# Gating unit's bias in two rounded parts, and the second layer's scan queries on 512 tokens, in a four-layer transformer kernel

## The reference, cut to what matters

```python
def sgu(pu, pv, ln_g, ln_b, w_s, b_s):
    vn = layer_norm(pv, ln_g, ln_b).reshape(B, nch, SGU_CHUNK, SGU_GROUPS, SGU_GROUP_DIM)
    mixed = jnp.einsum('gts,bnsgc->bntgc', w_s, vn) + b_s.T[None, None, :, :, None]
    return pu * mixed.reshape(B, N, SGU_WIDTH)

def gla_heads(...):
    q = heads(pq, GLA_DK) * (GLA_DK ** -0.5)
    k = heads(pk, GLA_DK)
...
    oc_f, s_f = gla_scan(qcg, kcg, vcg, gfc, zeros)
    ol_f, _ = gla_scan(qlg, klg, vlg, gfl, s_f)
```

## Time and profile before

| | |
|---|---|
| median of 3 runs | 3522.41 us (3520.08 to 3523.33) |
| the profiled execution: its time | 3518.86 us |
| its span, first to last instruction | 3516.7 us |
| mean granted clock of TensorE | 0.947 of full speed |
| TensorE busy | 3188.0 us, 91% of the span |
| VectorE, ScalarE, POOL busy | 54%, 34%, 6% |
| DMA | 321.84 MB, mean 92 GB/s |

### The profile page before, as it was taken

The page is one execution under the profiler, slowest core; times in us unless marked ns, Lnnn a source line. Parts: engine busy times, 40 slices in busy tenths (PEclk is TensorE's granted clock), DMA queues, the critical chain, the costliest instruction groups (busy, mean ns, idle before and its releaser), DMA issues.

```text
span 3516.7 us, 43743 instructions
## 1 busy us (share of the span) xinstructions
PE 3188.0 (91%) x18216; PEld 2645.0 (75%) x18216; DVE 1906.8 (54%) x2789; ACT 1178.4 (34%) x1763; POOL 208.4 (6%) x144
## 2 busy tenths in 40 slices
PE   7997889999988889999898999988998888997997
PEld 6886778888877667777777878756887777775776
DVE  7756555665434755777454443574434544457543
ACT  4234341221232544222342333253221534425322
POOL 0003100000010000000002120000001012100001
PEclk9999999999989999999899999999999799999997
DMA  5543123333211003555221123102113112320221
GB/s 203 178 154 126 55 78 126 121 131 120 84 55 60 1 13 121 179 176 177 88 86 69 65 75 110 42 1 81 54 66 96 71 66 88 103 81 7 97 94 58
DMA packets 91373, 321.84 MB, mean 92 GB/s; under 512 B 10070, under 2 KB 11991, under 8 KB 90025
## 3 DMA queue, kind: packets, MB, share of 16 engines
q1 hardware_dynamic: 81236, 289.43, 24.4%
q10 hardware_dynamic: 9940, 29.61, 2.3%
HBM read 297.26 MB, written 21.74 MB: 91 GB/s over the span
## 4 chain that ended last, share of the span: by engine, by line
PE 77%; DVE 10%; ACT 8%; issue 4%; DMA 1%; ACTq 0%; POOL 0%; SPq 0%; POOLq 0%; DVEq 0%
PE PS L384 76%; ACT whi L195 2%; ACT Pq L1274 1%; DVE STs L1311 1%; PE PS L387 1%; ACT nt L611 1%; DVE JUNK L514 1%; DVE stage L514 1%; DVE STq L1311 1%; DVE wlo L209 1%; ACT Ps L1274 1%; DMA Ht<-in_hT 1%; ACT U L616 0%; DVE fg L721 0%; ACT Ht L2304 0%
## 5 line engine op out<-in xcount | busy, mean ns | idle before, releaser
L384 PE MATMUL PS<-U,whi 128*128 128x512 f32 (+1 forms) x5408 | 1178.0, 363 | 93.7 <-DVE U L641 27.9
L384 PEld LDWEIGHTS PS<-U,whi 128*128 128x128 f32 x5408 | 913.8, 193 | 283.2 <-issue 59.3
L209 DVE TENSOR_TENSOR wlo<-stage,whi 128x1024 fp32r<-128x1024 f32 x339 | 417.0, 1232 | 1060.7 <-ACT whi L195 1060.1
L195 ACT ACTIVATE whi<-stage 128x1024 fp32r<-128x1024 f32 x339 | 358.3, 1058 | 1425.7 <-PE PS L384 1403.5
L384 PE MATMUL PS<-U,wlo 128*128 128x512 f32 (+1 forms) x2704 | 620.9, 355 | 0.0
L384 PE MATMUL PS<-Y,whi 128*128 128x512 f32 (+1 forms) x2240 | 582.9, 364 | 18.9 <-DVE Y L723 12.9
L384 PEld LDWEIGHTS PS<-U,wlo 128*128 128x128 f32 x2704 | 458.1, 189 | 79.7
L384 PEld LDWEIGHTS PS<-Y,whi 128*128 128x128 f32 x2240 | 397.3, 191 | 93.8 <-DVE Y L723 14.8
L384 PE MATMUL PS<-Y,wlo 128*128 128x512 f32 (+1 forms) x1120 | 367.7, 363 | 0.0
L384 PEld LDWEIGHTS PS<-Y,wlo 128*128 128x128 f32 x1120 | 208.9, 191 | 35.0
L384 PE MATMUL PS<-whi,U 128*128 128x512 f32 (+2 forms) x832 | 223.6, 359 | 11.3 <-DVE mV L1046 6.4
(11 more groups left out here) (412 smaller groups left out, 3279.3 us busy)
## 6 DMA issues: line engine op xcount, KB each, us to landing
stage<-in_w SPq DMA_DIRECT2D x128, 512.0 KB, 3.3
stage<-in_ada SPq DMA_DIRECT2D x80, 512.0 KB, 3.3
stage<-in_adb SPq DMA_DIRECT2D x48, 512.0 KB, 3.2
stage<-in_p_mg SPq DMA_DIRECT2D x16, 512.0 KB, 3.2
stage<-in_p_ma SPq DMA_DIRECT2D x16, 512.0 KB, 3.4
stage<-in_p_ms SPq DMA_DIRECT2D x16, 512.0 KB, 3.5
stage<-in_wo SPq DMA_DIRECT2D x16, 512.0 KB, 3.2
GS<-FS ACTq DMA_DIRECT2D x20, 384.0 KB
```

What stands on the lines that cost most here:

```text
L195: act.activation(self.parts[r % n][0], self.stage[i % len(self.stage)], ACT.Copy).then_inc(*self.S.up("w_hi", i))
L209: dve.tensor_tensor(lo, self.stage[i % len(self.stage)], hi.bitcast(F32), ALU.subtract).then_inc(*self.S.up("w_lo", i))
L384: return pe.matmul(o, l, r, start=start, stop=stop_, skip_group_check=True)
```

## The change

The bias is split once in each layer, into a rounded upper part (`BH`, by ScalarE) and the rest (`BL`, by VectorE); a row of ones is rounded too (`ONE`). The bias products then are taken over all four (or two) chunks of a bank at once, by a moving operand that repeats the group's 128 values: per group 2 + 2 rounded products of 512 and 256 columns in place of 6 plain ones of 128 in the first layer, and 2 of 512 in place of 4 in the second. The raw bias `B` moves to another place in memory. In the second layer, the query tiles j = 0 and 1 are projected and copied for 512 tokens, not 768.

```diff
@@ pe_gla @@
-                pe_proj(pe, T(f"p_gqk{L}", j), xU, True, ("g_qk", L, j))
+                pe_proj(pe, T(f"p_gqk{L}", j), xU, j >= 2 or G.full, ("g_qk", L, j))
@@ act_gla @@
-                act.activation(G.QK[:, j, :], B.of(i)[:, 0:TOK], ACT.Copy, scale=0.125 if j < 2 else 1.0).then_inc(
+                N = G.N if j < 2 else TOK
+                act.activation(G.QK[:, j, 0:N], B.of(i)[:, 0:N], ACT.Copy, scale=0.125 if j < 2 else 1.0).then_inc(
@@ Gating @@
-                self.B = place(n + "sb", [1, 4, 128], F32, offY2 + 18432)
+                self.BL = place(n + "sl", [1, 4, 128], F32R, offY2 + 18432)
+                self.B = place(n + "sb", [1, 4, 128], F32, offZ + 18432)[:, :, :]
+                self.BH = place(n + "sh", [1, 4, 128], F32R, offY2 + 20672)
+                self.ONE = place(n + "one", [1, 128], F32R, offY2 + 22720)
@@ pe_sgu @@
-                    pe.wait_ge(*at("sgu_in2", L))
+                    pe.wait_ge(*at("v_bias", L, 1))
+                    pe.wait_ge(*at("v_blo", L))
                 for c in range(G.nc):
                     mm(pe, s[:, 128 * c:128 * c + 128], G.V[:, c, 128 * g:128 * g + 128], G.W[:, g, :], c % 4 == 0, False)
-                    last = mm(pe, s[:, 128 * c:128 * c + 128], ONES[0:1, :], G.B[0:1, g, :], False, False)
+                for a, b in cols(G.full):
+                    for part in (G.BH, G.BL):
+                        last = mm(pe, s[:, a:b].rearrange("p (c e) -> p c e", e=128), G.ONE[0:1, :],
+                                  part[0:1, g:g + 1, :].to_broadcast([1, (b - a) // 128, 128]), False, part is G.BL)
@@ act_sgu @@
+            act.wait_ge(*at("sgu_in2", L))
+            act.activation(G.ONE[:, :], ONES[0:1, :], ACT.Copy).then_inc(*up("v_bias", L, 0))
+            act.activation(G.BH[:, :, :], G.B, ACT.Copy).then_inc(*up("v_bias", L, 1))
@@ dve_sgu @@
+            dve.wait_ge(*at("v_bias", L, 1))
+            dve.tensor_tensor(G.BL[:, :, :], G.B, G.BH[:, :, :].bitcast(F32), ALU.subtract).then_inc(*up("v_blo", L))
             dve.wait_ge(*at("w_used", T(f"p_sv{L}", 3)))
```

More of the change, by code:

```diff
@@ L52 @@
     "modulated": ("n_mul", "u_mod"), "gain": ("n_gain", "u_gain"), "rows_act": ("m_va", "g_va"),
-    "rows_dve": ("m_vd", "g_vd", "s_v", "q_v"), "v_norm": ("v_st", "v_ag", "v_rr", "v_n", "v_n1", "v_n2"),
+    "rows_dve": ("m_vd", "g_vd", "s_v", "q_v"), "v_norm": ("v_blo", "v_st", "v_ag", "v_rr", "v_n", "v_n1", "v_n2"),
     "qk_norm": ("q_rr", "q_nz"), "sigmoid": ("cb_sig", "cb_moved", "b_sig", "q_gs", "v_sig", "g_sig", "m_o"),
@@ L2520, in sp_program @@
                 sp.dma_start(V.W[:, :, :], A[f"sgu_w{L}"]).then_inc(*dma("sgu_in1", L))
-                sp.dma_start(V.B[:, :, :], A[f"sgu_b{L}"]).then_inc(*dma("sgu_in2", L))
+                sp.dma_start(V.B, A[f"sgu_b{L}"]).then_inc(*dma("sgu_in2", L))
                 sp_merge(sp, "s", L, N)
```

## The result

| | before | after |
|---|---|---|
| median, same chip | 3522.41 us (3518.55 to 3524.79, 5 runs) | 3496.17 us (3493.66 to 3500.01, 5 runs) |
| ratio | | 0.9927, 95% interval 0.9917 to 0.9938 |
| the profiled execution: its time | 3518.86 us | 3493.66 us |
| its span | 3516.7 us | 3491.7 us |
| mean granted clock | 0.947 | 0.951 |

A forecast was written before the change was run, and what follows sets the result against it. The prediction took TensorE's queue (77% of the chain) and its dipping clock as the bound. It summed 12.0 + 12.8 - 1.7 + 5.8 = 28.9 us, giving 3493.5 us from the median 3522.41, range 3485 to 3506.

The forecast's parts named there:

- small products at full clock: Gating units of both layers: cheaper bias products take 7.2 + 4.8 = 12.0 us off TensorE's queue.
- clock in the gating places: Half clock costs 15.9 us in four gating stretches; 12.8 us gained, with one fall left in the first layer's pair.
- wait behind the last pairs: Merge's fourth slice waits for VectorE's two serial groups: 0.7 us first layer unless a fall stays, 1.7 us second.
- query tiles: Second layer's scan start, j = 0 and 1: dropping the 256-column half saves 2.89 us twice, 5.8 us.
- untouched stretches: Elsewhere in the program: clock falls may shift either way by one or two of 3 us; not in the sum.
- I go by the row: Gating units: a removed plain product priced at the profile's 0.415 us, gaining 12.0 us, not 4.7 by the four-pass rule.
- the low bound: New one-row bias products priced like rounded products with 128 partitions: 0.234 us for 512 columns; high bound 0.99.
- The slower rival: One-partition rounded products run at the plain rate, 0.99 us for 512 columns: 3.6 us slower, 3526; chance 0.03.
- one fall of 3.1 us: First layer's last pair of groups: one clock fall assumed to remain, lowering the clock gain from 15.9 to 12.8 us.
- The rival in which the falls stay: Gating stretches: clock still falls as before, perhaps 5 of 15.9 us gained, 3500.6, at worst 3505; chance 0.28.
- The reason I gave, less time in small products: First layer's groups 0 and 1: 2.4 us of small products, down from 4.9, should no longer lower the clock.
- New work on ScalarE and VectorE: Bias copies and subtraction before the normalisation: cost nothing given 1.08 us of cover; under 1 us without it.

The follow-up runs named there:

- other profiles: The kernel before and the changed kernel, each run and profiled once more unedited: 3522.93 us and 3493.01 us.
- 64 rows in turn with 128: Kernel before, each bias product replaced by a plain 128-column product with a 64-row stationary operand, bias left out: 3510.1 us, one run.
- the rounded parts chunk by chunk: Changed kernel, its rounded bias parts added as two one-row products of 128 columns after each product with `V`: 3521.89 us, one run.
- The run with the moved group: Changed kernel, the third group's mixing product placed between the last group's two tiles in both layers: 3489.23 us, ratio to before 0.9899.
- the order alone: Kernel before, same plain products, but a group's bias products placed after all its products with `V`: 3501.97 us, ratio to before 0.9932.
- wide plain products: Kernel before, unrounded bias taken over four or two chunks per product, after the products with `V`: 3499.34 us, ratio to before 0.9932.

## Why the prediction was right, and where it was wrong

The direction, the time and the range held: 3496.2 us is 2.7 above the forecast, 26.2 us gained against 28.9. But the number is better than its terms, and that is in part luck: the small products and the clock gave 6.9 us more than forecast, the waits and the other stretches took 10.2 more. The measured terms below add to 25.4, and the two spans differ by 25.0. From the rows of the profile (waits counted from start to start):

| term | forecast, us | measured, us |
|---|---|---|
| small products at full clock | 12.0 | 10.2 + 6.3 = 16.5 |
| clock in the gating places | 12.8 | 15.2 |
| wait behind the last pairs | -1.7 | -1.9 - 2.3 |
| query tiles | 5.8 | 5.65 |
| untouched stretches, with the new wait of 0.6 | 0 | -7.7 (other profiles -4.9) |

- **The price of a product is the step that failed.** "I go by the row" priced the bias products at the 0.415 us between two starts, and left `V` at it. The row was right and its reading was not: 0.415 us was the price of a turn between 128 rows and one, paid by both products of the pair. With the turn gone a group saves 4.9 - 2.3 in the first layer and 3.22 - 1.64 in the second, four groups each. The rule set aside (the Trainium skill, FP8 and Floating Point Precision, TensorE Precision Notes: four passes for plain 32-bit) gave 0.234 us a product. The trace agrees once the products stand grouped: 1.43 us for six is 0.238. But its 4.7 us of gain would have been wrong too, since it prices no turn.
- **The new bias products** were taken at the low bound, 0.70 and 0.47 us a group. Measured are 0.89 and 0.65 (3322.46 to 3323.11). The low bound was the nearer one; what it left out are the two turns of a group, from 128 rows to one and back, about 0.1 us each. The slower rival at 0.99 us for 512 columns fell.
- **The clock.** I left one fall of 3.1 us in the first layer's pair; none came. The rival in which the falls stay fell with it. The reason I gave, less time in small products, is not what the runs show: 64 rows in turn with 128 kept the pace of before and had no fall, and the rounded parts chunk by chunk had one. The falls came in stretches with 128 rows and one row in turn, though not in all of them (the second layer's group 0 kept 1.00 before); why with that turn and not with the other is open.
- **A slip in the clock's sum.** The second layer's last pair ends with four slices, not three: its full-clock length was 3.2 + 3.3 + 4 x 0.70 = 9.3, not 8.6, so its fall cost 3.1, not 3.8. The four stretches then had 15.2 us to gain.
- **The new waits** came where they were put, with the releaser named, VectorE's subtraction. The first layer's was to be 0.7 with no fall left, and was 1.9; the second's 1.7, and was 2.3. The size hangs on TensorE's arrival, which was earlier, as the products were cheaper than forecast. VectorE's own times held: its two chains ended 7.87 us after the second pair's start, forecast 8.0. The run with the moved group shows that these waits are on the path.
- **The query tiles** passed in full: VectorE fell behind at j = 1 and caught up by j = 3, as argued. In the timeline of VectorE its weight subtraction starts late at 2775.00, right behind the scan, and at 2793.58 it waits again.
- **New work on ScalarE and VectorE** did cost something, 0.6 us, though less than the 1 us allowed. The prediction looked for the first tile to feel it in the second layer, where 1.08 us of cover were left and 0.48 remained (3315.39 to 3315.87). But in the first layer a tile had 0.06 us of cover (2484.86 to 2484.92 before), and now it has a marked wait of 0.51 us. All five profiles with the rounded bias have this wait, none of the seven with the plain bias or without one.
- **Untouched stretches** were only in the range's low end, as a shift "either way". They cost 5 to 8 us here, 0.6 of it the new wait. What decides where the falls come stays open; shown is that in the long stretch they came at the same places in two profiles of one kernel, and at other places in another kernel.

Of the change's two ideas in the bias, rounding and four chunks in a product, the second gives next to nothing by itself (49.71 and 34.66 us for the two gating places with the order alone, 49.62 and 34.60 with wide plain products) and the first 1.2 and 0.8 us (48.46 and 33.78 after). What gave the rest, 25.0 us, came along unasked: the order.

## What to carry to other kernels

Small products with stationary operands of unlike height belong in groups, all of one height and then all of the other; before pricing a product by the distance of two starts, look whether its neighbour sets that distance, and whether the weight load begins ahead of its product. After a gain on TensorE, read the chain in series that now arrives last, here VectorE's two last groups, and start its first link earlier. Judge a part of a change by the time between the same two instructions and not by the whole time alone, as one untouched stretch took 521 to 536 us in the profiles of these kernels, by its clock. Ahead of new work in a chain, look for the tile with the least cover in every layer, not only in one.

## What the runs showed of the hardware

- **Loads and row counts.** Plain products of 128 columns start 0.22 to 0.24 us apart when both stationary operands have 128 rows, with the load 0.11 us ahead of its product, and 0.415 us apart when rows go 128, 1, 128 or 128, 64, 128, with the load starting together with its product:

```profile
2511.01 0.30 PEld L384 LDWEIGHTS PS<-u0w,u0vn 128*128 128x128 f32 x2
```

This is before; the run with 64 rows reads the same. The Trainium skill (TensorE: Matmul & The Clock Gate, Part 3, what overlaps and what doesn't) has the load overlap a running product only when the row groups differ. The trace does not agree with the "only": here loads overlap with the same 128 rows in both operands, 0.11 us ahead, and do not where the counts differ but rows are shared. The measurement decides. (Under the mechanism, the same part also lets a load go ahead into a background weight buffer; whether that is what is seen here, no run shows.)
- **The clock fell while TensorE showed no idle time.** Group 0's stretch of before and that with rounded parts chunk by chunk are at 0.79 with busy time equal to the length (16.40 and 16.08 us); the one with 64 rows, its products 0.415 us apart as in before, is at 1.00.
- **A product of one row with a broadcast operand** runs at nearly the rate of a full one: 0.22 and 0.12 us for 512 and 256 columns between its own kind (2515.13 to 2515.35 to 2515.47), 0.33 to 0.34 when it is the first after 128 rows. The last one of a group, with 128 rows behind it, takes longer too: 0.21 us for 256 columns (2515.47 to 2515.68) and 0.32 for 512 (3322.79 to 3323.11). These two, 0.1 us each, are where 0.89 us instead of 0.70, and 0.65 instead of 0.47, come from.
- **One partition is as dear as 128** on ScalarE and VectorE: 0.62 us for 1 x 512 rounded, 0.67 us subtracted, against 0.63 and 0.69 for 128 x 512.
